# Delta rule in a hybrid block: the squared outputs split into two short-format parts, summed over features one tile later

## What is computed

```
u, w = sol[..., :Dv], sol[..., Dv:]
def step(S, inp):
    v_new = u_n - w_n @ S
    o = qd_n @ S + intra_n @ v_new
    S = S * exp(gl_n) + kd_n^T @ v_new
    return S, o
...
o = rms_norm(o, dn_out_norm_g[l]) * jax.nn.silu(z)      # mean of o*o over the head's 128 features
mix = jnp.concatenate([a_out, d_out], axis=-1)
x = x + jnp.einsum('bse,ed->bsd', mix, w_out[l])
```

## Time and profile before

| | |
|---|---|
| median of three runs | 1357.36 us (1355.74 to 1358.59) |
| the profiled execution | 1353.49 us, span 1351.8 us |
| PE matmul busy | 1284.9 us, 95% of the span |
| DVE busy | 736.3 us, 54% |
| ACT busy | 579.0 us, 43% |
| Pool busy | 750.1 us, 55% |
| mean granted clock of TensorE | 0.989 |
| PE waits for others in the delta-rule stage | 1.7 us for DVE's UT, 1.7 us for the load of UT, 2.5 us for DVE's sum of the attention's squares |

### The profile page before, as it was taken

One profiled execution on the slowest core, in us unless ns is written; L12 is line 12 of the kernel. 1 busy time (PEld: TensorE's weight loads), 2 busy tenths in 40 slices (PEclk: granted clock), 3 DMA queues, 4 the chain that ended last, 5 costly groups with the idle time before them and its releaser, 6 DMA issues.

```text
span 1351.8 us, 18274 instructions
## 1 busy us (share of the span) xinstructions
PE 1284.9 (95%) x6892; PEld 1069.6 (79%) x6892; DVE 736.3 (54%) x1030; ACT 579.0 (43%) x927; POOL 750.1 (55%) x516
## 2 busy tenths in 40 slices
PE   5999999999979989999988699999999999999999
PEld 5888888888867777888866488888888888788887
DVE  5456645536516757745486566554556566354552
ACT  5477645662126654552252232333332333364441
POOL 4322456643319992223067697887878984475541
PEclk9999999999989999999999799999999999999999
DMA  8311355431151004633020423444434436986563
GB/s 327 111 47 32 95 146 148 141 95 34 44 171 50 2 2 148 219 129 112 38 88 32 178 110 139 172 179 179 180 148 151 157 129 224 335 266 214 191 194 148
DMA packets 77807, 186.11 MB, mean 138 GB/s; under 512 B 20680, under 2 KB 24848, under 8 KB 70680
## 3 DMA queue, kind: packets, MB, share of 16 engines
q1 hardware_dynamic: 76368, 181.24, 39.5%
q10 hardware_dynamic: 1352, 3.70, 0.8%
HBM read 130.59 MB, written 56.94 MB: 139 GB/s over the span
## 4 chain that ended last, share of the span: by engine, by line
PE 71%; DVE 9%; ACT 5%; POOL 4%; DMA 4%; issue 3%; SPq 3%; DVEq 0%; ACTq 0%; POOLq 0%
PE ps L1938 27%; PE ps L337 14%; PE ps L1963 12%; PE ps L348 6%; POOL SX L811 3%; SPq L553 3%; PE ps L1770 2%; PE ps L1802 1%; DVE YB L1289 1%; DVE TMP L1286 1%; PE ps L1862 1%; PE ps L1785 1%; PE ps L322 1%; PE ps L1751 1%; DMA RAB<-down_t 1%
## 5 line engine op out<-in xcount | busy, mean ns | idle before, releaser
L337 PE MATMUL ps<-HT,SPLIT 128*128 128x512 f32 (+1 forms) x1488 | 329.7, 379 | 0.4 <-POOL SPLIT L287 0.4
L337 PEld LDWEIGHTS ps<-HT,SPLIT 128*128 128x128 f32 x1488 | 266.5, 190 | 49.7 <-issue 0.5
L1963 PE MATMUL ps<-S,HI 128*128 128x512 f32 x616 | 189.7, 389 | 1.3 <-POOL S L855 1.3
L855 POOL TENSOR_TENSOR S<-RAB,S 128x512 fp32r<-128x512 f32 x77 | 108.7, 1416 | 91.8 <-ACT S L1026 91.4
L285 POOL CAST SPLIT<-RAW 128x1024 fp32r<-128x1024 f32 x31 | 34.1, 1100 | 192.2 <-PE ps L337 186.8
L1963 PEld LDWEIGHTS ps<-S,HI 128*128 128x128 f32 x616 | 115.5, 188 | 25.5 <-issue 1.7
L1938 PE MATMUL ps<-HI,WR 128*128 128x512 f32 x360 | 116.7, 394 | 9.5 <-ACT UV L991 5.6
L1938 PE MATMUL ps<-S,WR 128*128 128x512 f32 x516 | 120.7, 389 | 1.6 <-DVE S L1413 1.6
L1963 PE MATMUL ps<-S,LO 128*128 128x512 f32 x308 | 119.8, 389 | 0.0
L1486 DVE TENSOR_TENSOR LO<-RAB,HI 128x512 fp32r<-128x512 f32 x77 | 65.2, 856 | 93.5 <-ACT HI L1023 93.4
L811 POOL TENSOR_SCALAR SX<-SX,row_inv 128x640 f32<-128x640 f32 (+4 forms) x64 | 95.7, 1513 | 34.8 <-DVE row_inv L1622 34.7
(11 more groups left out here) (259 smaller groups left out, 2493.1 us busy)
## 6 DMA issues: line engine op xcount, KB each, us to landing
hidden<-HB SPq DMA_DIRECT2D x11, 1792.0 KB, 6.7
RAB<-hidden SPq DMA_DIRECT2D x77, 256.0 KB, 3.1
RAW<-units SPq DMA_DIRECT2D x37, 512.0 KB, 4.1
RAWG<-w_gate SPq DMA_DIRECT2D x11, 1024.0 KB, 10.8
RAWU<-w_up SPq DMA_DIRECT2D x11, 1024.0 KB, 4.9
RAWD<-w_down SPq DMA_DIRECT2D x11, 1024.0 KB, 8.9
down_t<-RAWD SPq DMA_DIRECT2D x11, 1024.0 KB, 3.9
RAB<-down_t SPq DMA_DIRECT2D x44, 256.0 KB, 4.0
```

What stands on the lines that cost most here:

```text
L337: mm = pe.matmul(ps[:, bank + a // HALF, a % HALF:a % HALF + width], w, right[other][:, k, a:a + width], start=(k == 0 and part == 0 and o ...
L855: pool.tensor_tensor(down_b(q, 1), RAB[:, q % RAWS, 1, :], down_b(q, 0).bitcast(F32), ALU.subtract).then_inc(R["b_lo"], 1)
L1963: mm = pe.matmul(ps[:, bank + t, :], down_a(q, part)[:, t * P:(t + 1) * P], down_b(q, other), start=(p == 0 and i in (1, 6, 5, 7) and part ...
```

## The change

The squares of tile m's outputs are written by ACT twice: OSQ in float32, and OSH rounded to the short format. Pool writes their difference OSL. The sum over features is then two short-format matmuls (OSH, OSL) that add up in the same bank. PE does the sum of tile m-2 in round m, between the first level products and `dn_pe_ks(m-1)`; the sum of tile 6 stands before the last `dn_pe_ks`. ACT's Ln and Exp of tile m-2 move ahead of the copy and the squares of tile m-1. Pool's eight subtractions are placed in its order by hand: 0 and 1 before the split of unit 4, 2 to 4 behind it, 5 to 7 behind `mix_lo_of` 0 to 3 and before the split of unit 5. OSH and OSL take 4 KB per partition from a padding area.

```diff
+                def squares_lo(first, last):
+                    for m in range(first, last):
+                        pool.wait_ge(S["osq"], 2 * m + 2)
+                        ge(pool, S["osum"], m)
+                        pool.tensor_tensor(OSL[:, :, :], OSQ[:, :, :], OSH[:, :, :].bitcast(F32), ALU.subtract).then_inc(S["osl"], 1)
...
+                    if k == 4:
+                        squares_lo(0, 2)
+                    if k == 5:
+                        squares_lo(5, NT)
...
                     unit_split(pool, j % 2, j // 2 + 1, 0, j + 1, None if k < 2 else WO[:, WO_AT[k], :, :])
                     if k == 4:
+                        squares_lo(2, 5)
                         for i in range(4):
                             mix_lo_of(pool, i)
...
                 act.wait_ge(S["out_mm"], m + 1)
                 ge(act, S["osum"], m)
+                ge(act, S["osl"], m)
                 act.activation(OSQ[:, :, :], heads(dn_out_bank(m)), ACT.Square).then_inc(S["osq"], 1)
+                act.activation(OSH[:, :, :], heads(dn_out_bank(m)), ACT.Square).then_inc(S["osq"], 1)
...
                 for m in range(1, NT):
+                    if m >= 2:
+                        dn_act_scale(act, m - 2)
                     dn_act_new(act, m - 1)
                     dn_act_square(act, m - 1)
-                    dn_act_scale(act, m - 1)
                     if m in (5, 6):
...
+                dn_act_scale(act, NT - 2)
                 dn_act_new(act, NT - 1)
...
             def dn_pe_osum(pe, m):
-                pe.wait_ge(S["osq"], m + 1)
+                pe.wait_ge(S["osl"], m + 1)
                 ge(pe, S["oln"], m)
-                pe.matmul(ps[:, osum_bank(m), :], ones_r[:, :].bitcast(F32), flat(OSQ[:, :, :]), start=True, stop=True).then_inc(S["osum"], 1)
+                pe.matmul(ps[:, osum_bank(m), :], ones_r[:, :], flat(OSH[:, :, :]), start=True, stop=False)
+                pe.matmul(ps[:, osum_bank(m), :], ones_r[:, :], flat(OSL[:, :, :]), start=False, stop=True).then_inc(S["osum"], 1)
...
                     l_t(0, c)
+                if m >= 2:
+                    dn_pe_osum(pe, m - 2)
                 if m:
                     dn_pe_ks(pe, m - 1)
...
-                if m:
-                    dn_pe_osum(pe, m - 1)
...
                 last = NT - 1
+                dn_pe_osum(pe, last - 1)
                 dn_pe_ks(pe, last)
```

More of the change, by code:

```diff
@@ L187, in hymba_block @@
         dn_ring = ["KD", "NL", "UT", "IN", "KN", "TT"]
-        dn_layout = ([("pad_dn", [P, 7 * T + 4 * P], F32)] + [(n, [P, NHD, P], F32) for n in dn_one]
+        dn_layout = ([("pad_dn", [P, 6 * T], F32), ("OSH", [P, NHD, P], F32R), ("OSL", [P, NHD, P], F32R), ("pad_one", [P, 4 * P], F32)] + [(n, [P, NHD, P], F32) for n in dn_one]
                      + [(n, [P, 2, NHD, P], F32) for n in dn_ring])
@@ L200, in hymba_block @@
         BIAS, SX, PT = att
-        PP, VNEW, OSQ, ORS, STATE = dna[1:6]
-        KD, NL, UT, IN, KN, TT = dna[6:]
+        OSH, OSL = dna[1:3]
+        PP, VNEW, OSQ, ORS, STATE = dna[4:9]
+        KD, NL, UT, IN, KN, TT = dna[9:]
         WO = outs[0]
@@ L370, in hymba_block @@
               "pre_out", "keys_out", "block_out", "solve", "ks_mm", "r",
-              "new_mm", "new", "out_mm", "kv_mm", "st", "osq", "osum", "oln", "ors", "of", "mixed")}
+              "new_mm", "new", "out_mm", "kv_mm", "st", "osq", "osl", "osum", "oln", "ors", "of", "mixed")}
         rows_in = [sem("dn_rows_in0"), sem("dn_rows_in1")]
```

## The result

The changed kernel takes 1364.38 us in the median (1358.83 to 1366.88, nine runs) against 1355.75 us for the kernel before, run in turns with it (1352.51 to 1358.59, nine runs). The ratio is 1.0056, 95% interval 1.0039 to 1.0073: slower by about 7.6 us, which is also the difference of the two means (1363.52 and 1355.92); the medians lie 8.6 us apart. The profiled execution of the changed kernel took 1364.66 us, span 1362.9; that of before 1353.49, span 1351.8. So the profiles differ by 11.1 us, more than the timed runs do. The 3.5 us between them lie in which executions were profiled: that of before was 2.4 us quicker than the mean of its timed runs, that of the changed kernel 1.1 us slower than the mean of its own.

The account below looks back on a forecast made before the run. PE and DVE were taken to free each tile together, the old sum lying in a gap. Terms 2.25 + 1.3 + 5.0 + 0.6 - 0.4 = 8.75, with the clock 11.75, gave 1365.2 us profiled, 1369 median; range 1362 to 1373.

Parts of the forecast that it names:

- The old sum stood in a gap: Per tile, PE and DVE become free within 0.1 us; removing the old sum gives at most 0.1 us a tile.
- The moved sum, +0.45 in each of tiles 2 to 7: Between level products and `dn_pe_ks`, the sum is uncovered on the chain: +0.45 us per tile, 2.7 together.
- one of the six is hidden by the wait for UT: At tile 6's start, held 1.66 us by UT's load, one moved sum costs nothing; 2.25 us left.
- ACT's new order fits with 0.2 us to spare: On ACT, Ln, table load and Exp of tile m-2 end before the copy is wanted; no cost taken.
- the larger rival: On ACT, Ln and Exp end after the copy is wanted, adding about 5 us, so 1374; chance 0.06.
- the drain that the Trainium skill adds: 1380 ns at every ACT table switch; would make the copy 1.2 us late in six tiles, +7; not adopted.
- Tile 3, +1.3: Pool's subtractions block DVE's L1311 and then its gain product L1323 in tile 3: +1.3 us.
- Tile 7, 5.0 us: Tile 5's low part waits on Pool behind `mix_lo_of` 0 to 3, so PE stops 5.0 us in tile 7.
- The last tile, +0.6: The last sum comes directly before the last `dn_pe_ks` and waits for its low part: +0.6 us.
- The last sum's 0.4: The last sum stands among back-to-back projection matmuls, so its shortening gives 0.4 us back.
- The clock, two stretches of 1.5 us: After the tile 7 stop and the stop before tile 4, PE runs at half speed: about 1.5 us each, +3.0.
- The sum: All terms together: 8.75 us, with the clock 11.75; profiled execution 1365.2 us, median 1369.

Follow-up runs that it names:

- x later: Changed kernel with the four loads of x after the last tile's ring loads instead of after tile 5's; ratio to before 1.0046.
- the first four experiments: Changed kernel with tile 5's subtraction earlier on Pool, 1.0026; before with only the sum moved, 1.0030; split at the old place, 1.0015; changed with x loaded later, 1.0046.
- before with two waits out: Kernel before with the loads of x behind the last ring loads and unit 4's load two tiles later; 1350.49 us, ratio 0.9965.
- the kernel with the moved sum alone: Kernel before with only the float32 sum of tile m-2 moved before the product with the state, no split; ratio to before 1.0030.
- all waits out: Changed kernel with tile 5's subtraction before MIX low parts 2 and 3, x behind the last ring loads, unit 4's load two tiles later; ratio to before 0.9981.

## Why the prediction was right, point by point

- *The old sum stood in a gap.* Right, and the main point. PE waits 0.75 us in the emptied place, the moved float32 sum costs 0.85 a tile, and with both put together a quiet tile is longer by just the sum's length, so the place that it left was worth nothing. At the old place the shorter sum gained nothing either, but there PE waited for Pool.
- *The moved sum, +0.45 in each of tiles 2 to 7.* Right: quiet tiles take 10.07. That one of the six is hidden by the wait for UT was wrong. Tile 5 was to stay at 11.38 and took 12.22. I had tied UT's landing to the issue of x alone, which moved by 1.43 us. But the load of UT has a condition of its own, tile 5's `dn_pe_new`, and its issue moved by 1.88 (562.02 to 563.90): by the 1.43 and the moved sum's 0.45. The start of tile 6 moved by 2.26, so 0.38 came between issue and landing. Why is open; in the five profiles with x and unit 4 in their old places this time was 6.8 to 8.2 us.
- *ACT's new order fits with 0.2 us to spare.* Right (0.20), and the larger rival falls: Exp starts at 541.23, 0.01 after the end of its load at 539.94 + 1.28. So the drain that the Trainium skill adds (page "ScalarE: Activation LUTs", section "What ACT_TABLE_LOAD costs") does not show here, and the trace decides. DVE's product waits 0.42 us (0.47 worked out), and nothing comes of it.
- *Tile 3, +1.3.* Wrong in this profile, where it was -0.07; right as a mechanism. DVE's L1311 came where it was worked out (543.89 for 543.86), but Pool's L287 came at 544.02 and not near 543.6, because unit 4 landed later. The margin was 0.13 us, and in another execution of nearly the same order (x later) both products were blocked, with a wait of 3.35 us; tile 3 was longer there by 0.8 beside the moved sum, not by 1.3. It is a term that is there in some executions and not in others, and should have been given as that.
- *Tile 7, 5.0 us.* Right: 4.41 us as PE's wait, and 4.64 from where the sum would have stood (t0+0.89) to where it stood. The difference is that ACT's three instructions overlap by 0.1 each, which I had added end to end. E+8.0 was measured, E+8.4 worked out.
- *The last tile, +0.6.* Right (3.06 - 2.44 = 0.62). The last sum's 0.4 came back too: the first product of WO with LO behind it (L348, now L349) starts 13.15 us after the last product with the state and not 13.58 (613.24 - 600.09 and 602.38 - 588.80).
- *The clock, two stretches of 1.5 us.* The count and the size were right; the second place was tile 6 and not tile 4. The cost behind the stop was 3.90 - 2.38 = 1.52 us. The stop before tile 4 was 2.44 us and not about 4, since the collision took nothing more, and no slow clock followed it; the one in tile 6 followed a wait that the prediction had not lengthened.
- *The sum.* 11.75 worked out; 11.15 in the stretch, 11.1 in the spans. That it came so near is in part luck: tile 3 was put 1.4 us too high and tile 5 0.8 too low. Against the profiled execution the forecast of 1365.2 met 1364.66. The median was forecast at 1369 by putting the profile's difference on a median of three runs, 1357.36, and is 1364.38. This last step was mis-sized. The profiled execution of before was a quick one (1353.49; one of its nine timed runs is lower; its clock, 0.989, is near the top of the 0.982 to 0.990 in the 32 runs of this kernel beside the first four experiments), while that of the changed kernel lies 0.3 us above its median, so their difference is larger than that of typical runs. The median of before, too, is 1355.75 with nine runs, not 1357.36.
- *The spread.* The nine runs of the changed kernel spread over 8.1 us, and the longer ones have the lower clock: 0.989 in the run of 1358.83 us, 0.980 in that of 1366.88. So slow-clock stretches carry a part of the spread. They are not the change's own: the 32 runs of before spread over 10.8 us, and one wait ahead of the stretch, the same in every kernel, was followed by the slow clock in some profiles only (last section). The twelve runs of before with two waits out spread over 3.8 us. Which waits do it in the timed runs isn't shown, since only one execution of each kernel was profiled.

## What to carry to other kernels

Shortening an instruction on the busiest engine is worth nothing where it stands in a gap, and moving it onto the chain costs its whole length, however short it has become. An in-order engine needs its queue read to the end: a 1.3 us subtraction placed behind two others, which wait for a third engine, stopped TensorE for 4.4 us in one tile of eight. Taking out one wait can lengthen the next: the load that was moved away from Pool's collision came into the queue ahead of x, and the wait for UT grew from 1.66 to 3.81 us. So test such edits together.

## What the runs showed of the hardware

A wait's length alone did not decide whether TensorE's clock fell to 1.2 GHz. In the windows behind the waits it fell after 2.08, 2.90, 3.31, 3.35, 3.81, 4.41 and 5.03 us, and it did not after 2.12 us (tile 4 of the kernel with the moved sum alone), 2.44 us (tile 4 of the changed kernel, the next tile at 10.07) and 2.65 us. The plainest case is PE's wait in tile 0, ahead of the stretch, for DVE's sum of the attention's squares: 2.50 or 2.51 us in all ten profiles. Timelines of PE, the changed kernel and then the one with all waits out:

```profile
510.53 3.55 PE L1869 MATMUL ps<-PROJ,ones_r 128*128 128x512 f32 x4 [2.51 <-DVE PROJ L1334]
```

```profile
510.19 1.98 PE L1871 MATMUL ps<-PROJ,ones_r 128*128 128x512 f32 x4 [2.51 <-DVE PROJ L1336]
```

The same four matmuls take 1.98 us at a clock of 1.00 in four of the ten, and 2.53 to 3.78 us in the other six, where the clock of the 3 us from their start is 0.50 to 0.72. Both kernels, before and changed, are among the six. Where two tiles of the stretch can be compared a fall cost 1.46 to 1.65 us, so a wait near this length costs that much more in some executions.

Where Pool reads two operands from SBUF, a DVE instruction with two SBUF operands that starts behind it is held. DVE's L1311 (L1313, L1327 or L1329 in other kernels) started 0.23 to 1.78 us behind Pool's L287 or L288 in tile 3 or 5 of six profiles; it took 1.14 to 2.67 us instead of 0.68, and each time ended 0.54 to 0.56 us after Pool's. Started 0.13 and 0.17 us ahead of it, or 0.01 behind, DVE's took 0.68 us, and Pool's took 2.72 to 2.90 instead of 2.36. So the order is decided by tenths of a microsecond. The Trainium skill's rule (page "SBUF — State Buffer", section "Who interferes with whom"), by which the engine that issues first has the shared pair for its whole instruction and the other is blocked, agrees. DVE's state update, which takes one operand from PSUM, kept its 1.11 us beside Pool's subtraction in tile 3 of the changed kernel.
